# Two latents and two quarters of the tokens turned in 32x32 blocks by VectorE through DRAM instead of by TensorE

## The chip, the cores and the metric

One core of a Trainium2 chip runs the whole layer. The time is the device time in microseconds (us) of one execution, and a version's time is the median over its runs. In the text "the matrix engine" is TensorE (PE in the profile), VectorE is DVE, ScalarE is ACT, GpSimd is POOL and SyncE is SP.

## The reference, cut to what matters

One layer over 256 tokens (SEQ) of width 2048 in float32: a projection, two mixers side by side, a projection back, and a SwiGLU block.

```python
h    = rms_norm(x, attn_norm_w)
proj = h @ w_in                              # hq, hf, hi, hg (4 x 1024), c_q (512), c_kv (512), k_r (64)
o_a  = hgrn2_mixer(hq, hf, hi, hg, ...)      # gated linear recurrence, 8 heads of 128
q    = rms_norm(c_q, q_norm_w) @ w_uq        # the first latent, 256 x 512
kv   = rms_norm(c_kv, kv_norm_w) @ w_ukv     # the second latent, 256 x 512
o_b  = attention(q, kv, k_r)                 # 8 heads, rotary part from the positions
x    = x + concat([o_a, o_b]) @ w_out
h    = rms_norm(x, ffn_norm_w)
gate, up = split(h @ w_gate_up)              # 2 x 5632 columns
x    = x + (silu(gate) * up) @ w_down
```

## The kernel before

Tokens lie on the 128 partitions in two tiles (NT = 2, P = 128). A matrix product needs its token operand the other way round, features on partitions, so every activation that is multiplied has to be turned. The operands are split in two float32r parts, hi and lo, and a product is hi x hi + lo x hi + hi x lo: three matmuls per tile.

The weights come in **granules**: 256 weight rows by up to 512 columns, through a ring of four slots (`raw`). SP loads a granule, ACT makes `w_hi` (`convert`, L805), DVE makes `w_lo` (L1132), PE multiplies (L1751, L1754). 137 granules of the mixer and of `w_out` come first (G0 = 137), then the FFN, whose first block (16 granules, positions 137 to 152) still goes by the same loop; from the second block on it is a loop of another form.

The order of all work beside the granules is a table, `schedule()`: pairs of a position and a step. Each engine runs the same loop over positions g. ACT and DVE first convert granule g + 3 and then do their part of the steps at g; PE does its part of the steps at g and then multiplies granule g. So each engine is a strict queue, and ACT's cast of granule n waits until PE has finished granule n - 4 (the slot of `w_hi`). Turned tokens go through `SPLITS`, in schedule order: ACT makes the hi part and counts `s_thi`, DVE makes the lo part and counts `s_tlo`, and PE waits for `s_tlo`.

The steps that matter here, with their places:

- blocks of the mixer, in granules: lat (0 to 24), hq0 (25 to 32), uq0 (33, 34), hf0 (35 to 42), ukv0 (43, 44). `uq` multiplies the first latent, `ukv` the second; `split_needed` says what each block waits for.
- `lat_a`, `lat_b` (i = 0, 1): ACT squares a latent (L827), DVE takes mean and root and multiplies the latent by the result (L1260). `lat_in` copies the latent out of PSUM on DVE (L1253).
- `lat_t` (i, j): PE turns two blocks of 128 features for both tiles, four transposes against the identity (`turn_x`, L1793) into a PSUM bank, ACT and DVE split them into `mT_hi` and `mT_lo` (L852, L1153). Two such steps per latent, at positions 26 and 30.
- `angles` (DVE, about 20 small operations from L1194 to L1218) and `sines` (ACT, L870, with a table load before and one after) make the rotary factors, at positions 29 and 30.
- `hq` (ACT, L941): the first block read out of PSUM at position 33, again between two table loads. hf0 multiplies into the same banks and waits for it.
- `kr_b`, `q_a`, `q_b`, `q_t`: rotary key, norm and rotation of the first query block on DVE at 34 to 36; PE turns its result at position 39 (L1815), waiting for `s_stage`.
- `out1`, `out2` (c = 0 to 3): DVE adds the two parts of the `w_out` product to X (L1480). `out2` of quarter c (512 features) has two granules, and its addition stands at position 131 + 2c.
- `sq2`: ACT squares the quarter. `x2` (c, j): PE turns two blocks of the quarter, four transposes; ACT and DVE split them into `hT_hi` and `hT_lo`. Two such steps per quarter, at 133, 135, 137 and 139. Before the transposes PE waits until DVE has read `out2` of that quarter.

`hidden`, the result of an FFN block, is already turned another way: DVE turns 32x32 blocks (`turn_hidden`, L1533), POOL writes them to DRAM (`move_out`, L761) and reads them back in four DMAs (`move_in`, L767), one per row of blocks, so that the blocks come to their places.

```python
for g, (b, k, n) in enumerate(GRANULES):        # PE
    for s in steps_at(g):
        step(s)
    ...
    pe.wait_ge(s_tlo, split_needed(g))
    ...
    multiply(g % RING, g, lhs_of(kind, ks), 0, len(rows) - 1, main[b % 2], cols, ks)
```

Of the kernel before, what the change touches and what calls it, by code (L numbers as in the profile page):

```python
# [31 lines left out]
P = 128  # L32
# [182 lines left out]

Q = 32
# [3 lines left out]
def schedule():  # L220
# [52 lines left out]
    for c in range(4):  # L273
        s += [(END[("out1", c)], ("out1", c)), (END[("out2", c)], ("out2", c)), (END[("out2", c)] + 1, ("sq2", c))]
# [22 lines left out]
def side_uses(step):  # L297

    kind = step[0]
    if kind in ("x2", "lat_t", "o_t"):  # L300
        return [(step, "dve")]
# [24 lines left out]
SPLITS = [step for _, step in SCHEDULE if step[0] in ("x", "x2", "lat_t", "o_t", "attend")]  # L326
# [16 lines left out]
def split_needed(g):  # L343
# [5 lines left out]
    if kind == "uq":  # L349
        return SPLIT[("lat_t", 0, 1)] + 1  # L350
    if kind == "ukv":
        return SPLIT[("lat_t", 1, 1)] + 1
# [7 lines left out]
def hybrid_layer(nc, x, columns, positions, w_in, hgrn_lb, w_uq, w_ukv, q_head_norm_w, k_head_norm_w, w_out, w_gate_up,  # L360
# [7 lines left out]
    with ExitStack() as ctx:  # L368
# [80 lines left out]
        latents = (lat, hv)  # L449
        qTn = X[:, 0, :].rearrange("p (h t) -> p h t", h=HEADS)  # L450
# [8 lines left out]
        hiddenT = sb("hiddenT", [P, P // Q, SEQ])  # L459
        squares = nc.dram_tensor("squares", (P // Q, Q, P // Q, SEQ), F32, kind="Internal").ap()  # L460
# [17 lines left out]
        def turned(t):  # L478
            return hiddenT[:, :, :].rearrange("p a (t k r) -> p t k a r", t=NT, r=Q)[:, t, :, :, :]
# [24 lines left out]
        s_lat = sem("s_lat")  # L504
        s_sq = sem("s_sq")
# [18 lines left out]

        s_turned = sem("s_turned")
# [93 lines left out]
        def _(sp):  # L619
# [22 lines left out]
            for j in range(GU):  # L642
                half, k = divmod(j, KT // 2)
                slot = (G0 + j) % RING
# [47 lines left out]
        def _(pool):  # L692
# [57 lines left out]

            pool.wait_ge(s_lbused, 1)
# [4 lines left out]
            pool.dma_start(X[:, :, :], x_v).then_inc(s_xagain, 16)  # L756

# [38 lines left out]
        def _(act):  # L796
# [58 lines left out]
            def step(s):  # L855
# [26 lines left out]
                elif kind == "lat_t":  # L882
                    i, j = a
                    ps, k, col = filled(s), 4 * i + 2 * j, (V_KVN if i else V_QN) + 2 * j
                    split_hi([(mT_hi[:, k + n, :], ps[:, n * SEQ:(n + 1) * SEQ], col + n) for n in range(2)])
# [46 lines left out]
                elif kind in ("hq", "hf_a", "hi", "hg"):  # L932
# [3 lines left out]
                    if kind == "hq" and not a[0]:  # L936
                        act.wait_ge(s_side, USE[("lat_t", 0, 1)] + 1)
# [61 lines left out]
                elif kind == "x2":  # L999
                    ps, k = filled(s), 4 * a[0] + 2 * a[1]  # L1000
                    split_hi([(hT_hi[:, k + n, :], ps[:, n * SEQ:(n + 1) * SEQ], V_FFN + k + n) for n in range(2)])
                elif kind == "r2b":
                    root(("r2a",), NT)
# [115 lines left out]
        def _(dve):  # L1119
# [100 lines left out]
            def step(s):  # L1220
# [40 lines left out]
                elif kind == "lat_t":  # L1261
                    i, j = a
                    ps, k, col = filled(s), 4 * i + 2 * j, (V_KVN if i else V_QN) + 2 * j
                    split_lo(s, [(mT_lo[:, k + n, :], ps[:, n * SEQ:(n + 1) * SEQ], mT_hi[:, k + n, :], col + n)
                                 for n in range(2)])
# [204 lines left out]
                elif kind in ("out1", "out2"):  # L1470
# [7 lines left out]
                    for t in range(NT):  # L1478
                        v = X[:, t, c * NB:(c + 1) * NB]
                        tt(v, v, ps[t][:, :], ALU.add).then_inc(read, 1)  # L1480
                elif kind == "x2":
# [75 lines left out]
            def sum_ff_tokens():  # L1557
# [7 lines left out]
                dve.wait_ge(s_tlo, SPLIT[("x2", 0, 1)] + 1)  # L1565
# [171 lines left out]
        def _(pe):  # L1737
# [58 lines left out]
            def step(s):  # L1796
# [6 lines left out]
                elif kind == "lat_t":  # L1803
                    i, j = a
                    pe.wait_ge(s_const, N_IDENT)
                    pe.wait_ge(s_lat, NT * (i + 1))
                    turn_x(s, 2 * j, latents[i])
# [114 lines left out]

            for g, (b, k, n) in enumerate(GRANULES):
# [12 lines left out]
            for j in range(GU):  # L1936
# [3 lines left out]
                pe.wait_ge(s_tlo, SPLIT[("x2",) + divmod(min(j, 7), 2)] + 1)  # L1940
# [158 lines left out]
```

## Time and profile before

| | |
|---|---|
| median of three runs | 1108.75 us (1108.43 to 1109.88) |
| the profiled execution | 1108.98 us, its span 1107.3 us, so 1.7 us lie around the span |
| busy in the span | PE 1098.5 us (99%), DVE 899.7 (81%), ACT 644.6 (58%), POOL 60.3 (5%) |
| granted clock of PE | 1.00 throughout |
| DMA | 232 MB, mean 210 GB/s |

The page gives the busy time of each engine, the span in 40 slices, and the chain that ended last. The timeline lists single instructions with the idle time of their engine before them and what ended it; a row that stands for several instructions gives their count and the time from the first start to the last end. A PE row overlaps its successor: a granule's length is read from start to start.

### The profile page before, as it was taken

To read this page: it belongs to the slowest core of one execution; us is meant where nothing else is said; L and a number is where in the kernel's file an instruction comes from. 1 tells how busy PE (TensorE), PEld (TensorE's weight loads), DVE (VectorE), ACT (ScalarE), POOL (GpSimd) and SP (SyncE) were. 2 spreads that over 40 slices of the span, in tenths; PEclk is the share of its full clock that TensorE was granted. 3 is DMA by queue.
4 is the path that set the end of the run, shared out by engine and by line. 5 is a ranking of instruction groups with operands and counts; after the bars stand their busy time and mean duration, and the time that the engine had idled before them with its cause. 6 is when DMAs were issued, how large, how long until landed. Compare 5 with 4: busy or idle time off the path is not lost.

```text
span 1107.3 us, 15268 instructions
## 1 busy us (share of the span) xinstructions
PE 1098.5 (99%) x5142; PEld 924.2 (83%) x5142; DVE 899.7 (81%) x1237; ACT 644.6 (58%) x907; POOL 60.3 (5%) x154
## 2 busy tenths in 40 slices
PE   8999999999999999999999999999999999999998
PEld 7988888888888888888888888888888888888887
DVE  6688787587876576688888888988988889999887
ACT  6676776668654465355455455554554555654553
POOL 1500000000000000101100000010010010000000
PEclk9999999999999999999999999999999999999999
DMA  9966455555655465767777777777777787766665
GB/s 308 288 182 207 127 169 169 147 160 157 228 172 185 158 180 165 237 216 213 242 234 225 237 235 212 237 236 225 229 235 231 236 251 231 229 214 207 196 203 171
DMA packets 107411, 232.11 MB, mean 210 GB/s; under 512 B 8288, under 2 KB 17248, under 8 KB 107104
## 3 DMA queue, kind: packets, MB, share of 16 engines
q1 hardware_dynamic: 101360, 211.34, 61.3%
q0 software_dynamic: 5856, 19.93, 6.0%
q8 instruction: 28, 0.46, 0.2%
q10 hardware_dynamic: 144, 0.20, 0.1%
q14 instruction: 23, 0.19, 0.1%
HBM read 220.94 MB, written 10.49 MB: 209 GB/s over the span
## 4 chain that ended last, share of the span: by engine, by line
PE 93%; DVE 3%; DMA 2%; issue 1%; ACT 1%; SPq 0%; DVEq 0%; ACTq 0%
PE side L1979 22%; PE main L1751 22%; PE side L1981 11%; PE main L1754 11%; PE side L1949 4%; PE side L1950 4%; PE side L1951 4%; PE main L1951 3%; PE main L1949 3%; PE main L1950 3%; DMA raw<-in_w_down 1%; PE main L1771 1%; DVE w_lo L1590 1%; PE side L1877 1%; PE side L1793 1%
## 5 line engine op out<-in xcount | busy, mean ns | idle before, releaser
L1021 ACT CAST w_hi<-raw 128x1024 fp32r<-128x1024 f32 x245 | 239.6, 984 | 160.3 <-PE side L1979 61.1
L1590 DVE TENSOR_TENSOR w_lo<-raw,w_hi 128x1024 fp32r<-128x1024 f32 x245 | 274.5, 1133 | 17.1 <-ACT w_hi L1021 17.1
L1132 DVE TENSOR_TENSOR w_lo<-raw,w_hi 128x1024 fp32r<-128x1024 f32 (+3 forms) x156 | 178.9, 1156 | 96.1 <-ACT w_hi L805 94.5
L805 ACT CAST w_hi<-raw 128x1024 fp32r<-128x1024 f32 (+3 forms) x155 | 153.2, 997 | 127.2 <-PE main L1751 117.7
L1751 PE MATMUL main<-w_hi,hT_hi 128*128 128x512 f32 (+2 forms) x416 | 161.1, 388 | 0.0
L1754 PE MATMUL main<-w_hi,hT_lo 128*128 128x512 f32 (+2 forms) x416 | 157.6, 380 | 0.0
L1979 PE MATMUL side<-w_hi,hT_hi 128*128 128x512 f32 x400 | 155.6, 389 | 0.0
L1981 PE MATMUL side<-w_hi,hT_lo 128*128 128x512 f32 x400 | 155.6, 389 | 0.0
L1751 PE MATMUL main<-w_lo,hT_hi 128*128 128x512 f32 (+2 forms) x416 | 107.2, 379 | 0.0
L1979 PE MATMUL side<-w_lo,hT_hi 128*128 128x512 f32 x400 | 106.9, 389 | 0.0
L1754 PEld LDWEIGHTS main<-w_hi,hT_lo 128*128 128x128 f32 x416 | 78.2, 188 | 12.9
L1751 PEld LDWEIGHTS main<-w_hi,hT_hi 128*128 128x128 f32 x416 | 78.2, 188 | 12.9
L1751 PEld LDWEIGHTS main<-w_lo,hT_hi 128*128 128x128 f32 x416 | 76.8, 188 | 14.1
L1979 PEld LDWEIGHTS side<-w_hi,hT_hi 128*128 128x128 f32 x400 | 75.1, 188 | 15.6
L1979 PEld LDWEIGHTS side<-w_lo,hT_hi 128*128 128x128 f32 x400 | 75.1, 188 | 15.6
L1981 PEld LDWEIGHTS side<-w_hi,hT_lo 128*128 128x128 f32 x400 | 75.1, 188 | 15.5
L1590 DVE TENSOR_TENSOR w_lo<-last_two,w_hi 128x1024 fp32r<-128x1024 f32 x39 | 47.8, 1225 | 40.6 <-ACT w_hi L1021 40.5
L1021 ACT CAST w_hi<-last_two 128x1024 fp32r<-128x1024 f32 x39 | 41.1, 1053 | 64.5 <-PE side L1979 64.5
L1021 ACT CAST w_hi<-first_two 128x1024 fp32r<-128x1024 f32 x39 | 41.2, 1056 | 59.2 <-PE side L1979 57.3
L1979 PE MATMUL side<-w_hi,aT_hi 128*128 128x512 f32 x184 | 71.6, 389 | 0.0
L1981 PE MATMUL side<-w_hi,aT_lo 128*128 128x512 f32 x184 | 71.6, 389 | 0.0
L1751 PE MATMUL main<-w_hi,mT_hi 128*128 128x512 f32 (+1 forms) x160 | 62.0, 387 | 0.0
(295 smaller groups left out, 1877.1 us busy)
## 6 DMA issues: line engine op xcount, KB each, us to landing
raw<-in_w_gate_up SPq DMA_DIRECT2D x176, 512.0 KB, 4.8
raw<-in_w_down SPq DMA_DIRECT2D x88, 512.0 KB, 4.6
raw<-in_w_in SPq DMA_DIRECT2D x64, 512.0 KB, 4.3
raw<-in_w_out SPq DMA_DIRECT2D x32, 512.0 KB, 3.7
raw<-in_w_in SPq DMA_DIRECT2D x15, 384.0 KB, 5.5
squares<-hiddenT POOLq DMA_DIRECT2D x11, 512.0 KB, 5.2
hiddenT<-squares POOLq DMA_DIRECT2D x44, 128.0 KB, 5.4
raw<-in_w_ukv SPq DMA_DIRECT2D x8, 512.0 KB, 4.3
```

Of the source, the lines that this page charges most:

```text
L805: copy(w_hi[:, slot, 0:n], raw[:, slot, 0:n]).then_inc(s_hi, 1)
L1021: copy(w_hi[:, n % RING, 0:cols], src).then_inc(s_hi, 1)
L1132: tt(w_lo[:, slot, 0:n], raw[:, slot, 0:n], w_hi[:, slot, 0:n].bitcast(F32), ALU.subtract)\
L1590: tt(w_lo[:, n % RING, 0:cols], src, w_hi[:, n % RING, 0:cols].bitcast(F32), ALU.subtract)\
L1751: m = matmul(banks[t][:, 0:cols], hi[:, at[n], tok], rhs, start=(part == "hi" and k == k_first), stop=(part == "lo" and k == last))
L1754: matmul(banks[t][:, 0:cols], lo[:, at[n], tok], rhs, start=False, stop=False)
L1771: m = matmul(banks[t][:, 0:cols], tokens[:, k, t * P:(t + 1) * P], w[:, slot, n * cols:(n + 1) * cols], start=(part == "hi" and k == 0), s ...
L1949: matmul(bank, hi, big, start=first, stop=False)
L1950: matmul(bank, lo, big, start=False, stop=False)
L1951: return matmul(bank, hi, small, start=False, stop=last)
L1979: m = matmul(bank, hi, rhs, start=False, stop=(part == "lo" and (t, half) in last))
L1981: matmul(bank, lo, rhs, start=False, stop=False)
```

## The change

Four of the eight groups of eight transposes leave PE: both latents, and quarters 0 and 1 of the FFN's tokens. DVE turns them in 32x32 blocks out of SBUF, POOL writes the blocks to DRAM and reads them back in four DMAs, and ACT and DVE make hi and lo from SBUF instead of PSUM. The FFN's first block takes its quarters in the order 2, 0, 1, 3.

```diff
+FF_ORDER = [(c, n) for c in (2, 0, 1, 3) for n in range(2)]
...
-        s += [(e + 1, ("lat_a", i)), (e + 2, ("lat_b", i))] + [(e + 5, ("lat_t", i, n)) for n in range(2)]
+        s += [(e + 1, ("lat_a", i)), (e + 2, ("lat_b", i)), (e + 2, ("lat_turn", i))]
+        s += [(30 + n if i == 0 else 34, ("lat_back", i, n)) for n in range(2)]
...
-    s += [(END[("out2", c)] + 2, ("x2", c, n)) for c in range(4) for n in range(2)]
+    s += [(END[("out2", c)], ("x_turn", c)) for c in range(2)]
+    s += [(e + 2 * c, ("x_back", c, n)) for c in range(2) for n in range(2)]
+    s += [(e - 1 if c == 2 else e + 2, ("x2", c, n)) for c in range(2, 4) for n in range(2)]
...
     if kind == "uq":
-        return SPLIT[("lat_t", 0, 1)] + 1
+        return SPLIT[("lat_back", 0, 1)] + 1
...
+            for i in range(2):                                              # POOL
+                pool.wait_ge(s_latturned, i + 1)
+                pool.dma_start(lat_scratch[i].rearrange("a c b x -> (a c) b x"), latents_in_blocks[i])\
+                    .then_inc(s_latout[i], 16)
+                pool.wait_ge(s_latout[i], 16)
+                for b in range(P // Q):
+                    pool.dma_start(latents_in_blocks[i][Q * b:Q * (b + 1), :, :],
+                                   lat_scratch[i][:, :, b, :].rearrange("a c x -> c a x")).then_inc(s_latback[i], 16)
...
+            for c in range(2):
+                pool.wait_ge(s_xturned, NT * (c + 1))
+                pool.dma_start(x_scratch[c].rearrange("a c b x -> (a c) b x"), in_blocks(c)).then_inc(s_xout[c], 16)
+            for c in range(2):
+                pool.wait_ge(s_xout[c], 16)
+                for b in range(P // Q):
+                    pool.dma_start(in_blocks(c)[Q * b:Q * (b + 1), :, :],
+                                   x_scratch[c][:, :, b, :].rearrange("a c x -> c a x")).then_inc(s_xback[c], 16)
...
+                elif kind == "lat_back":                                    # ACT
+                    i, j = a
+                    act.wait_ge(s_latback[i], MOVED)
+                    src = latents_in_blocks[i].rearrange("p a (t k r) -> p k t a r", t=NT, r=Q)
+                    split_hi([(mT_hi[:, 4 * i + k, :].rearrange("p (t a r) -> p t a r", t=NT, r=Q), src[:, k, :, :, :],
+                               (V_KVN if i else V_QN) + k) for k in (2 * j, 2 * j + 1)])
...
+                elif kind == "lat_turn":                                    # DVE
+                    i = a[0]
+                    dve.wait_ge(s_lat, NT * (i + 1))
+                    nc.vector.transpose(latents_in_blocks[i].rearrange("p b (n r) -> p n b r", r=Q),
+                                        latents[i][:, :, :].rearrange("p t (k b c) -> p (t k) b c", b=P // Q, c=Q))\
+                        .then_inc(s_latturned, 1)
...
+                elif kind == "x_turn":                                      # DVE
+                    ...
+                    for t in range(NT):
+                        nc.vector.transpose(in_blocks(c).rearrange("p b (t k r) -> p t k b r", t=NT, r=Q)[:, t, :, :, :],
+                                            X[:, t, c * NB:(c + 1) * NB].rearrange("p (k b c) -> p k b c", b=P // Q, c=Q))\
+                            .then_inc(s_xturned, 1)
```

`x_back` is to a quarter what `lat_back` is to a latent. DVE's part of both makes four operations of 128x128 per step where `lat_t` and `x2` made two of 128x256. The blocks of the latents lie in `hkT` and `hgate`, those of the quarters in `hiddenT` and `hidden`. The wait of PE for the identity moves to the start of its loop.

**Where the instructions stand.** DVE around the first latent, positions 23 to 26 (`lat` is the first latent, `hv` the place of the second), before:

```order
L1260 TENSOR_SCALAR lat<-lat,opening 128x512 x2
L1132 TENSOR_TENSOR w_lo<-raw,w_hi 128x1024 x2
L1253 COPY hv<-main 128x256
L1251 TENSOR_SCALAR krw<-main,opening 128x64
L1253 COPY hv<-main 128x256
L1251 TENSOR_SCALAR krw<-main,opening 128x64
L1132 TENSOR_TENSOR w_lo<-raw,w_hi 128x1024
L1153 SCALAR_TENSOR_TENSOR mT_lo<-side,opening,mT_hi 128x256 x4
```

and with the change:

```order
L1305 TENSOR_SCALAR lat<-lat,opening 128x512 x2
L1309 STREAM_TRANSPOSE hkT<-lat 128x8x4x32
L1177 TENSOR_TENSOR w_lo<-raw,w_hi 128x1024 x2
L1298 COPY hv<-main 128x256
L1296 TENSOR_SCALAR krw<-main,opening 128x64
L1298 COPY hv<-main 128x256
L1296 TENSOR_SCALAR krw<-main,opening 128x64
L1177 TENSOR_TENSOR w_lo<-raw,w_hi 128x1024
```

The turning stands ahead of two weight granules and of the copies of the second latent; the lo part of the first latent is gone from here. The same turning of the second latent comes after its own multiplication.

ACT around the sines, positions 30 and 31 (the first two `mT_hi` rows of the change are `lat_back` of the first latent, halves 0 and 1), before:

```order
L805 CAST w_hi<-raw 128x768
L852 ACTIVATE mT_hi<-side,opening 128x256 x4
L870 ACT_TABLE_LOAD
L870 ACTIVATE sincos<-sincos 128x128
L844 ACT_TABLE_LOAD
L805 CAST w_hi<-raw 128x768
L805 CAST w_hi<-raw 128x1024 x2
```

and with the change:

```order
L842 CAST w_hi<-raw 128x768
L889 ACTIVATE mT_hi<-hkT,opening 128x256 x2
L907 ACT_TABLE_LOAD
L907 ACTIVATE sincos<-sincos 128x128
L881 ACT_TABLE_LOAD
L842 CAST w_hi<-raw 128x768
L889 ACTIVATE mT_hi<-hkT,opening 128x256 x2
L842 CAST w_hi<-raw 128x1024 x2
```

Before, these four made the second latent, needed at granule 43, and the first had been done at position 26; now they make the first latent, needed at granule 33, and its second half stands behind the sines and a cast. The second latent follows after `hq0`.

DVE at the end of `w_out`, positions 131 to 137, with the change (X additions are `out2` of quarters 0 to 3):

```order
L1539 TENSOR_TENSOR X<-X,main 128x512 x2
L1545 STREAM_TRANSPOSE hiddenT<-X 128x4x4x32 x2
L1177 TENSOR_TENSOR w_lo<-raw,w_hi 128x1024 x2
L1539 TENSOR_TENSOR X<-X,main 128x512 x2
L1545 STREAM_TRANSPOSE hidden<-X 128x4x4x32 x2
L1177 TENSOR_TENSOR w_lo<-raw,w_hi 128x1024 x2
L1539 TENSOR_TENSOR X<-X,main 128x512 x2
L1177 TENSOR_TENSOR w_lo<-raw,w_hi 128x1024
L1198 SCALAR_TENSOR_TENSOR hT_lo<-side,opening,hT_hi 128x256 x4
L1177 TENSOR_TENSOR w_lo<-raw,w_hi 128x1024
L1539 TENSOR_TENSOR X<-X,main 128x512 x2
L1557 SCALAR_TENSOR_TENSOR hT_lo<-hiddenT,opening,hT_hi 128x128 x8
```

The lo part of quarter 2 (`hT_lo<-side`) now comes one granule after the addition of that quarter, where before two `w_lo` and the addition of quarter 3 stood between.

## Rows read from the trace of the kernel before

**Rows 1.** The page, busy time of each engine, its share and instructions.
```profile
PE 1098.5 (99%) x5142; PEld 924.2 (83%) x5142; DVE 899.7 (81%) x1237; ACT 644.6 (58%) x907; POOL 60.3 (5%) x154
```
**Rows 2.** The waits of PE: line, for what; us in total, times, longest.
```profile
PE main L1771 <- ACTq L1058: 4.5, 1, 4.5
```
**Rows 3.** Timeline of PE: start us, us, line, instruction, tiles, count.
```profile
57.35 1.04 PE L1793 MATMUL side<-ident,lat 128*128 128x128 f32 x8
...
60.99 0.39 PE L1751 MATMUL main<-w_hi,hT_hi 128*128 128x512 f32 x1
...
78.21 0.33 PE L1751 MATMUL main<-w_hi,mT_hi 128*128 128x384 f32 x1
...
93.32 0.60 PE L1815 MATMUL side<-ident,stage 128*128 128x128 f32 x4
...
400.30 0.39 PE L1751 MATMUL main<-w_hi,hT_hi 128*128 128x512 f32 x1
...
403.02 1.03 PE L1793 MATMUL side<-ident,X 128*128 128x128 f32 x8
```
**Rows 4.** Instructions of L1533: duration ns min/median/max, first and last start.
```profile
L1533 DVE STREAM_TRANSPOSE hiddenT<-hidden x11: 1236/1239/1241, 457.3 to 881.2; 128x1024 f32<-128x1024 f32 x11
```
**Rows 5.** Timeline of DVE from the first latent to the sines.
```profile
55.07 0.88 DVE L1260 TENSOR_SCALAR lat<-lat,opening 128x512 f32<-128x512 f32 x2
...
58.14 0.42 DVE L1253 COPY hv<-main 128x256 f32<-128x256 f32 x1
...
60.32 0.88 DVE L1153 SCALAR_TENSOR_TENSOR mT_lo<-side,opening,mT_hi 128x256 fp32r<-128x256 f32 x2
...
65.32 0.88 DVE L1260 TENSOR_SCALAR hv<-hv,opening 128x512 f32<-128x512 f32 x2
...
67.77 1.22 DVE L1132 TENSOR_TENSOR w_lo<-raw,w_hi 128x1024 fp32r<-128x1024 f32 x1 [0.43 <-ACT w_hi L805]
68.91 0.16 DVE L1194 CAST pos_f<-pos_i 128x2 f32<-128x2 int32 x1
...
73.46 0.23 DVE L1218 TENSOR_SCALAR sincos<-sincos 128x128 f32<-128x128 f32 x1
73.60 0.95 DVE L1132 TENSOR_TENSOR w_lo<-raw,w_hi 128x768 fp32r<-128x768 f32 x1
```
**Rows 6.** Timeline of ACT from the second latent's squares to after `hq0`.
```profile
59.99 0.74 ACT L827 ACTIVATE hlf<-hv,opening 128x512 f32<-128x512 f32 x1
...
62.34 1.04 ACT L805 CAST w_hi<-raw 128x1024 fp32r<-128x1024 f32 x1
...
70.15 1.56 ACT L852 ACTIVATE mT_hi<-side,opening 128x256 fp32r<-128x256 f32 x4
...
74.04 1.28 ACT L844 ACT_TABLE_LOAD   x1
75.34 1.79 ACT L805 CAST w_hi<-raw 128x768 fp32r<-128x768 f32 x2
78.46 1.05 ACT L805 CAST w_hi<-raw 128x1024 fp32r<-128x1024 f32 x1 [1.34 <-PE main L1751]
...
83.41 2.00 ACT L805 CAST w_hi<-raw 128x1024 fp32r<-128x1024 f32 x2
```
**Rows 7.** Timeline of DVE from the granule after `uq0` to the first queries.
```profile
84.48 1.23 DVE L1132 TENSOR_TENSOR w_lo<-raw,w_hi 128x1024 fp32r<-128x1024 f32 x1 [2.75 <-ACT w_hi L805]
...
92.52 0.28 DVE L1188 TENSOR_TENSOR stage_r<-rot 128x128 f32<-128x128 f32 x1
```
**Rows 8.** Timeline of POOL at one turning of `hidden`, and landing times of these DMAs.
```profile
458.89 0.57 POOL L761 DMA_DIRECT2D squares<-hiddenT  x1 [169.34 <-DVE hiddenT L1533]
464.16 2.21 POOL L767 DMA_DIRECT2D hiddenT<-squares  x4 [4.70 <-DMA squares<-hiddenT]
...
DMA to landing us min/median/max: 3.6/5.3/7.8
```
**Rows 9.** Timeline of DVE, the addition of quarter 2.
```profile
405.50 1.28 DVE L1480 TENSOR_TENSOR X<-X,main 128x512 f32<-128x512 f32 x2
```

More of the change, by code:

```diff
@@ L299, in side_uses @@
     kind = step[0]
-    if kind in ("x2", "lat_t", "o_t"):
+    if kind in ("x2", "o_t"):
         return [(step, "dve")]
@@ L324 @@
             GIVEN[USE[_key]] = _given[_engine]
-SPLITS = [step for _, step in SCHEDULE if step[0] in ("x", "x2", "lat_t", "o_t", "attend")]
+SPLITS = [step for _, step in SCHEDULE if step[0] in ("x", "x2", "x_back", "lat_back", "o_t", "attend")]
 SPLIT = {step: n for n, step in enumerate(SPLITS)}
@@ L449, in hybrid_layer @@
         latents = (lat, hv)
+        latents_in_blocks = [v[:, :, :].rearrange("p t c -> p (t c)").rearrange("p (a x) -> p a x", a=P // Q)
+                             for v in (hkT, hgate)]
         qTn = X[:, 0, :].rearrange("p (h t) -> p h t", h=HEADS)
@@ L504, in hybrid_layer @@
         s_lat = sem("s_lat")
+        s_latturned = sem("s_latturned")
+        s_latout = [sem(f"s_latout{i}") for i in range(2)]
+        s_latback = [sem(f"s_latback{i}") for i in range(2)]
         s_sq = sem("s_sq")
@@ L523, in hybrid_layer @@
         s_join = sem("s_join")
+        s_xturned = sem("s_xturned")
+        s_xout = [sem(f"s_xout{c}") for c in range(2)]
+        s_xback = [sem(f"s_xback{c}") for c in range(2)]
         s_turned = sem("s_turned")
@@ L643, in _ @@
                 half, k = divmod(j, KT // 2)
+                k = 2 * FF_ORDER[k][0] + FF_ORDER[k][1]
                 slot = (G0 + j) % RING
@@ L1260, in step @@
                         ts(v, v, inv[:, t:t + 1], None, ALU.mult).then_inc(s_lat, 1)
-                elif kind == "lat_t":
-                    i, j = a
-                    ps, k, col = filled(s), 4 * i + 2 * j, (V_KVN if i else V_QN) + 2 * j
-                    split_lo(s, [(mT_lo[:, k + n, :], ps[:, n * SEQ:(n + 1) * SEQ], mT_hi[:, k + n, :], col + n)
-                                 for n in range(2)])
+                elif kind == "lat_turn":
[4 more added lines that the diff above has]
+                        .then_inc(s_latturned, 1)
+                elif kind == "lat_back":
+                    i, j = a
+                    dve.wait_ge(s_latback[i], MOVED)
+                    dve.wait_ge(s_thi, SPLIT[s] + 1)
+                    src = latents_in_blocks[i].rearrange("p a (t k r) -> p k t a r", t=NT, r=Q)
+                    for k in (2 * j, 2 * j + 1):
+                        col = (V_KVN if i else V_QN) + k
+                        for t in range(NT):
+                            hi, lo = [v[:, 4 * i + k, t * P:(t + 1) * P].rearrange("p (a r) -> p a r", r=Q)
+                                      for v in (mT_hi, mT_lo)]
+                            ins = stt(out=lo, in0=src[:, k, t, :, :], scalar=vec_cols[:, col:col + 1],
+                                      in1=hi.bitcast(F32), op0=ALU.mult, op1=ALU.subtract)
+                    ins.then_inc(s_tlo, 1)
                 elif kind == "kr_b":
```

60 lines of the change are left out of this document (41 added, 19 removed).

## The prediction

> **What bounds the kernel now.** I read the page first: PE is busy 1098.5 of 1107.3 us [rows 1], and of the 8.8 us that are left, 4.5 are its one real wait, for the first operands [rows 2]. So PE is the bound from end to end: what leaves its queue shortens the kernel by its own length, unless PE then arrives at something that isn't ready. The second reading is therefore not "who is busy" but "how much earlier than PE is each result there", and that takes the timelines of PE, DVE, ACT and POOL at the two places of the change [rows 3 to 9].
>
> **What is removed.** A granule that follows eight transposes starts 3.64 us after they start (57.35 to 60.99), one without them is 2.72 us long (400.30 to 403.02) [rows 3]. A group of eight costs 0.92 us. Four groups go: 2 x 0.92 = 1.84 us in the mixer, 1.84 us before the FFN, 3.7 us in all. That is the whole gain: 0.33% of the time.
>
> The Trainium skill ("VectorE: DVE Perf Modes", "The three transpose paths" and "Rules for kernel authors") speaks against the change: VectorE turns 32x32 blocks only, and a full 128x128 transpose belongs on TensorE where PSUM can take it. The rows agree on the durations: eight blocks take 1.24 us on DVE [rows 4] and 0.92 on PE. By the rule alone the sum would be four times 0.32, 1.3 us slower; by the rows what counts is whose queue is the bound, and where the new results are waited for.
>
> **The mixer, step by step.** I carry the times of the trace forward; up to 55.95, the end of the first latent's multiplication [rows 5], nothing differs.
> 1. DVE turns the first latent, same shape as the `hidden` block: 1.24 us [rows 4], to 57.2. Behind it stand two w_lo of 1.14 each (67.77 to 68.91) and the copies of the second latent (58.14 to 60.32 less one w_lo, 1.05) [rows 5]: copies done at 60.6, 1.3 us later than before.
> 2. ACT's squares of the second latent need these copies. They started at 59.99, held back until then by the hi part of the first latent that now is gone; now they start at 60.6, and the cast behind them at 62.95 instead of 62.34 [rows 6]. DVE waits for that cast, so the second latent's multiplication ends at 66.8 instead of 66.2 [rows 5].
> 3. DVE turns the second latent, 1.24 us, to 68.1; two w_lo to 70.3. The angles started at 68.91 and ran to 73.69 (73.46 + 0.23), 4.78 us [rows 5]. Now: 70.3 to 75.1, 1.4 us late. The lo part that left this stretch (twice 0.88 [rows 5]) had mostly stood in time in which DVE waits for casts anyway.
> 4. ACT's sine waits for the angles; from their end to the next cast passed 1.65 us (73.69 to 75.34: sine and a table load [rows 5, 6]). So that cast starts at 76.7. It is the cast of `uq0`'s second granule, and the second half of the first latent stands behind it on both engines. Its hi part follows 0.75 us behind that narrow cast and costs half of the four of the second latent, 0.86 us [rows 6]: 78.35. On DVE w_lo of 768 columns (0.95 [rows 5]) comes first, from 77.5 to 78.4, then the lo part, for which I take the 0.88 of the pair it replaces [rows 5]: 79.35.
> 5. PE reached `uq0` at 78.21 [rows 3], and would now at 76.37. It waits for the lo part until 79.35: **3.0 us of stall**, more than both groups of transposes gave.
> 6. Then the second latent, now behind `hq0`. ACT: hi to 78.3, one cast (0.95) to 79.25, then the 4.95 us from cast to cast across `hq0` (78.46 to 83.41 [rows 6]), so the cast of granule 37 starts at 84.2 and ends at 85.25. From this granule's w_lo to the first query block DVE ran without a pause, 84.48 to 92.80 [rows 7], 8.32 us; now the lo parts of the second latent are in it, 2 x 0.88. The block is there at 95.3. PE's transposes of it came 15.1 us after `uq0` (78.21 to 93.32 [rows 3]): 94.45. **Another 0.9 us.**
>
> Mixer: -1.84 + 3.0 + 0.9 = +2.1 us.
>
> The way through DRAM isn't on this path. `hidden` was turned at 458.54 (457.3 [rows 4] + 1.24); the write was issued at 458.89, the reads from 464.16 to 466.37, the last of them some 0.55 before that end [rows 8]. With the median of 5.3 us for its landing a latent is back 12.6 us after its turning: the first at 69.8, the second at 80.7. ACT needs the first by 72.9 (0.9 of hi and 1.3 of table load before the sine at 75.1), the second by 85. In POOL's queue they stand right after the masks of the opening, and nothing else waits behind them before the recurrence. SP's queue is untouched, and the added traffic, 0.5 MB out and 0.5 MB back per latent, meets loads that land well ahead of their casts: ACT waits for PE there, not for DMA [rows 6].
>
> What the operations from SBUF cost isn't in the trace. From below I set half of the replaced pair, from above the double: a stall of 2.1 to 4.7 us at `uq0`. I take the replaced rows, equal in elements.
>
> **Before the FFN.** DVE's additions of a quarter end 3.76 us after PE has started the granule behind the quarter: 405.50 + 1.28 = 406.78 against 403.02 [rows 3, 9]. ACT's cast (it waits for PE's slot), w_lo and the two additions make that up, and the change leaves them as they are; the turnings of quarters 0 and 1 come one position earlier, in time where DVE waited. But quarter 2's transposes now stand one granule after the quarter, 2.72 us, not two. PE waits until the additions are done: **1.05 us of stall**. With it, quarter 2 is split in time: PE needs it 3.6 us after the transposes start, and four transposes (0.5), hi (0.86), lo (0.88) and the steps between the engines take some 2.6.
>
> Quarter 0, counted from the start of granule 133: turned (1.25 us after its addition) at -0.4, written by 5.2; POOL first sends quarter 1 (turned at 5.0), then issues the reads from 5.9 to 8.1, landed by 12.9. PE starts granule 137 at 12.85 (four granules, the stall, one group of transposes), and ACT has a cast and two squares before it: about 15.7. Quarter 1 is written by 10.7, back at 17.6, and ACT comes to it near 21. Both hidden, with 2.8 us of room. PE's sum tiles use quarter 0 alone, much later.
>
> Before the FFN: -1.84 + 1.05 = -0.8 us. The reordered quarters load the same bytes, and the identity is made long before PE's first matmul: both nothing.
>
> **Sum.** +2.1 - 0.8 = +1.3 us on the profiled execution's 1108.98, so 1110.3; that execution lies 0.2 above the median of its runs, so 1110.0 for a median. Its own range, from the bounds above: with the cheap SBUF operations 1108.2 (both stalls of the mixer shrink, the second to nothing), with the dear ones 1111.8. A measurement of this kernel can tell about 0.2%, 2.2 us, from no change: 1106.5 to 1111.0 is "the same".
>
> **Rivals.**
> - *All of it comes through*: 1108.75 - 3.7 = 1105.1. For it: PE has no wait anywhere now, DVE still waits 0.43 us for a cast in this very stretch [rows 5] and is only 81% busy. Against it: PE arrives 1.84 us earlier at everything, while sine and angles are later by 1.4. And even with the latents for nothing, the mixer can't give it: from the cast at 76.7 ACT has two casts and, from the second on, 3.65 us to the end of the `hq0` read (78.46 to 83.41 less a table load of 1.30 [rows 6]), done 82.05, and hf0 (82.44 before, 93.32 less four granules) can't start sooner, 80.6 being PE's time. That would be 1107.5. 0.12 for a gain of over 2.2.
> - *The latent comes back late.* Such DMAs land in 3.6 to 7.8 us [rows 8]. If write and last read both take 7.8, the first latent is back at 74.8 instead of 69.8. ACT, which stands at it with sine, table load and cast queued behind, then gets to the sine at 77.0 instead of 75.1, and `uq0` waits 1.9 us more: 1111.9, slower. It decides from 72.9 on, and costs its own lateness from there; 73.9 makes it measurable. For it: two DMAs one after the other, beside the weights' queue. Against: the median gives 3 us of room. 0.12.
> - *The forecast*: 0.76, of which 0.08 lie above 1111.0 (the dear SBUF operations).
>
> So faster 0.12, same 0.68, slower 0.20. The range of 8 in 10 reaches from 1107.0, below which only the first rival lies, to 1112.2, which holds the second.
>
> **What would show it.** In the profile of the changed kernel, PE has three new waits where it had none: about 3 us at the first matmul on `mT_hi` (`uq0`, near 76.4) for DVE's `mT_lo`, about 0.9 at the query transposes for `stage_r`, about 1 before the transposes of X for DVE's addition. The angles end near 75.1, ACT's `mT_hi` rows from `hkT` take 0.4 to 0.5 us each, and the first of them doesn't wait for a DMA. Transposes drop from 8 groups of x8 on L1793's successor to 4 (the two of the recurrence's output stay beside the two quarters). I am wrong if PE runs into `uq0` without a wait, or if ACT waits for `hkT`'s DMA past 73, or if a stall turns up where I have none, at hf0 or at the FFN's third granule.

## The result, and the profile after

| | before | after |
|---|---|---|
| median of the timed runs | 1108.97 us (8 runs, 1108.43 to 1109.88) | 1113.03 us (8 runs, 1110.98 to 1115.08) |
| profiled execution, its span | 1108.98, 1107.3 us | 1113.29, 1111.5 us |

The ratio is 1.0033, with a 95% interval of 1.0024 to 1.0042. The changed kernel is slower by 0.33%, or 3.7 us (4.1 between the medians), where the forecast had 1.3, and the median lies 0.8 us above the upper end of the range.

The first look is at the busy times on the page; they answer to [rows 1]. PE's 32 transposes are gone, and it is busy for as long as before, in a longer span:

```profile
PE 1098.4 (99%) x5110; PEld 924.5 (83%) x5110; DVE 906.6 (82%) x1259; ACT 646.0 (58%) x907; POOL 71.2 (6%) x174
```

So what left PE's queue came back as slower matmuls. The second look is at PE's waits (line, for what; us in total, times, longest), against [rows 2]:

```profile
PE main L1850 <- ACTq L1103: 4.4, 1, 4.4
PE main L1830 <- DVE mT_lo L1322: 3.1, 1, 3.1
PE side L1872 <- DVE X L1539: 0.9, 1, 0.9
PE main L1850 <- ACT hT_hi L889: 0.7, 1, 0.7
```

The second row is the forecast's wait at `uq0`, the third its wait ahead of quarter 2. The forecast's wait at the query transposes is not there. To see where the 4.2 us of span come from, I took the start of the same instruction in both traces at five points, and the end of both spans; the column "later by" is the difference.

| point | before | after | later by |
|---|---|---|---|
| first matmul after the opening (granule 9) | 23.88 | 26.00 | 2.12 |
| first matmul of `uq0` | 78.21 | 81.73 | 3.52 |
| first matmul of `hf0` | 82.39 | 87.60 | 5.21 |
| query transposes | 93.32 | 98.52 | 5.20 |
| table load of the FFN's first Silu | 434.25 | 438.78 | 4.53 |
| end of the span | 1107.3 | 1111.5 | 4.2 |

**Two things the forecast hadn't.** One lies ahead of everything the change touches. The timeline of PE in the opening of the changed kernel (start us, us, line, instruction, tiles, count):

```profile
7.76 0.84 PE L1850 MATMUL main<-w_lo,hT_hi 128*128 128x384 f32 x2
9.28 1.62 PE L1850 MATMUL main<-w_hi,hT_hi 128*128 128x384 f32 x4 [0.68 <-ACT hT_hi L889]
10.69 1.49 PE L1850 MATMUL main<-w_hi,hT_lo 128*128 128x384 f32 x4
11.97 1.49 PE L1850 MATMUL main<-w_lo,hT_hi 128*128 128x384 f32 x4
13.25 1.10 PE L1850 MATMUL main<-w_hi,hT_hi 128*128 128x384 f32 x4
14.19 0.88 PE L1850 MATMUL main<-w_hi,hT_lo 128*128 128x384 f32 x4
```

and the same stretch before:

```profile
7.94 0.82 PE L1771 MATMUL main<-w_lo,hT_hi 128*128 128x384 f32 x2
8.96 0.94 PE L1771 MATMUL main<-w_hi,hT_hi 128*128 128x384 f32 x4 [0.20 <-ACT hT_hi L852]
9.78 0.97 PE L1771 MATMUL main<-w_hi,hT_lo 128*128 128x384 f32 x4
10.59 0.85 PE L1771 MATMUL main<-w_lo,hT_hi 128*128 128x384 f32 x4
11.28 0.85 PE L1771 MATMUL main<-w_hi,hT_hi 128*128 128x384 f32 x4
```

Four matmuls take 1.28 us from start to start (10.69 to 11.97), and 0.69 before (10.59 to 11.28): 0.32 us for 384 columns against 0.173. These are the two levels of the clock, 1.2 and 2.4 GHz. Both kernels start at the lower one; after, PE stays on it some 4 us longer. The Trainium skill ("TensorE: Matmul & The Clock Gate", Part 1: The HAM clock gate) says that the length of the slow start differs from run to run of one kernel; whether that is so here is for the runs below to tell.

The other is behind the wait at `uq0`. PE's timeline there (the wait is in brackets):

```profile
81.73 0.45 PE L1830 MATMUL main<-w_hi,mT_hi 128*128 128x384 f32 x1 [3.06 <-DVE mT_lo L1322]
...
83.58 0.52 PE L1830 MATMUL main<-w_hi,mT_hi 128*128 128x384 f32 x1
83.90 0.52 PE L1833 MATMUL main<-w_hi,mT_lo 128*128 128x384 f32 x1
84.22 1.43 PE L1830 MATMUL main<-w_lo,mT_hi 128*128 128x384 f32 x4
85.48 0.34 PE L1830 MATMUL main<-w_hi,mT_hi 128*128 128x384 f32 x1
...
87.60 0.39 PE L1830 MATMUL main<-w_hi,hT_hi 128*128 128x512 f32 x1
```

The first granule of `uq0` takes 3.75 us (81.73 to 85.48), the second 2.12. Before, the two took 4.18 together (78.21 to 82.39); now 5.87. The granted clock says why; the windows of that stretch, whose columns are PE, weight loads, DVE, ACT and POOL busy, the clock, DMA share and GB/s:

```profile
76.00:78.60 2.60, 2.60 (x12) 1.88 (x10) 2.50 (x8) 1.42 (x2) 1.08 (x2) 1.00 0.96 264
78.60:81.70 3.10, 0.07 (x1) 0.00 (x0) 2.47 (x8) 3.09 (x6) 0.00 (x0) 1.00 0.65 190
81.70:85.40 3.70, 3.67 (x12) 3.67 (x13) 3.67 (x5) 3.65 (x5) 0.00 (x0) 0.54 0.84 238
85.40:88.00 2.60, 2.60 (x15) 2.56 (x15) 1.18 (x2) 2.59 (x5) 0.00 (x0) 0.99 0.50 143
```

0.54 behind the wait, 1.00 ahead of it. The wait costs its 3.06 us and then another 1.69 (5.87 less 4.18).

**The chain that makes the wait is the forecast's.** The timelines of DVE and ACT, to be held against [rows 5, 6]; 2.1 us of each start are the opening's:

```profile
72.33 0.16 DVE L1239 CAST pos_f<-pos_i 128x2 f32<-128x2 int32 x1
...
76.88 0.26 DVE L1263 TENSOR_SCALAR sincos<-sincos 128x128 f32<-128x128 f32 x1
...
79.65 0.96 DVE L1177 TENSOR_TENSOR w_lo<-raw,w_hi 128x768 fp32r<-128x768 f32 x1 [0.63 <-ACT w_hi L842]
80.53 1.14 DVE L1322 SCALAR_TENSOR_TENSOR mT_lo<-hkT,opening,mT_hi 128x128 fp32r<-128x128 f32 x4
```

```profile
72.21 0.84 ACT L842 CAST w_hi<-raw 128x768 fp32r<-128x768 f32 x1 [3.27 <-DMA raw<-in_w_uq]
...
77.17 0.31 ACT L907 ACTIVATE sincos<-sincos 128x128 f32<-128x128 f32 x1 [2.01 <-DVE sincos L1263]
77.50 1.28 ACT L881 ACT_TABLE_LOAD   x1
78.79 0.83 ACT L842 CAST w_hi<-raw 128x768 fp32r<-128x768 f32 x1
79.53 0.91 ACT L889 ACTIVATE mT_hi<-hkT,opening 128x256 fp32r<-128x256 f32 x2
```

The angles start at 70.2 when the 2.12 of the opening are taken off (forecast 70.3), end at 75.0 (75.1), the cast starts at 76.7 (76.7) and the lo part ends at 79.5 (79.35). The way through DRAM is hidden: no row of PE, ACT or DVE in the mixer waits for `hkT` or `hgate` from DRAM (in a second profile of this kernel ACT waits 0.22 us for `hkT`, ahead of 2.79 us for the angles). But a cast waits 3.27 us for its load, where ACT in the trace of before waited for PE; it costs nothing, since ACT waits another 2.01 for the angles behind it.

### The profile page after: what moved, and what is told of

Same layout as the page of the kernel before. It is cut to its first block, busy times and chain, and to the rows that moved or that the text cites. A ratio compares the mean times of both kernels' runs of the same rounds, so it can differ in the third digit from the quotient of the medians.

```text
span 1111.5 us, 15220 instructions
## 1 busy us (share of the span) xinstructions
PE 1098.4 (99%) x5110; PEld 924.5 (83%) x5110; DVE 906.6 (82%) x1259; ACT 646.0 (58%) x907; POOL 71.2 (6%) x174
## 4 chain that ended last, share of the span: by engine, by line
PE 91%; DVE 4%; ACT 2%; issue 1%; DMA 0%; SPq 0%; DVEq 0%; ACTq 0%
PE side L2057 24%; PE main L1830 19%; PE side L2059 12%; PE main L1833 9%; PE side L2027 4%; PE side L2028 4%; PE side L2029 4%; PE main L2029 3%; PE main L2027 3%; PE main L2028 3%; PE main L1850 2%; DVE w_lo L1177 1%; PE side L1951 1%; ACT w_hi L842 1%; DMA x_columns<-in_columns 0%
## 5 line engine op out<-in xcount | busy, mean ns | idle before, releaser
L1177 DVE TENSOR_TENSOR w_lo<-raw,w_hi 128x1024 fp32r<-128x1024 f32 (+3 forms) x156 | 178.5, 1154 | 95.3 <-ACT w_hi L842 94.2
L2057 PEld LDWEIGHTS side<-w_hi,hT_hi 128*128 128x128 f32 x400 | 75.1, 188 | 15.6
L2057 PEld LDWEIGHTS side<-w_lo,hT_hi 128*128 128x128 f32 x400 | 75.1, 188 | 15.6
L2059 PEld LDWEIGHTS side<-w_hi,hT_lo 128*128 128x128 f32 x400 | 75.1, 188 | 15.6
```

The source lines that it names most:

```text
L1177: tt(w_lo[:, slot, 0:n], raw[:, slot, 0:n], w_hi[:, slot, 0:n].bitcast(F32), ALU.subtract)\
L2057: m = matmul(bank, hi, rhs, start=False, stop=(part == "lo" and (t, half) in last))
L2059: matmul(bank, lo, rhs, start=False, stop=False)
```

## The experiments

Every time is compared with runs of the kernel before on the same chip. "later by" is as above, the start of an instruction less that in the profile of before.

**The two parts apart, and the wait that moved.** Four kernels: the latents alone (`x2` and the FFN's order as before), the quarters alone (`lat_t` as before), and PE's wait for the identity, which the change puts at the start of PE's loop, elsewhere:

```diff
-            pe.wait_ge(s_const, N_IDENT)
             for g, (b, k, n) in enumerate(GRANULES):
...
                 elif kind in ("q_t", "k_t"):
                     j, b = a[0], int(kind == "k_t")
+                    pe.wait_ge(s_const, N_IDENT)
```

and in the fourth the kernel before with that wait moved to the start of the loop. Latents alone:

> Only the two latents are turned by VectorE; X, the FFN's order and the position of quarter 2 are as before. Theory: the mixer alone loses 3.1 us (1.84 us of transposes gone, 3.2 of wait at uq0, 1.7 because TensorE works at the lower clock level behind that wait), so 3.1 us above the kernel before where PE's ninth granule starts as early as there (23.9 us), and 2.1 more in runs where the opening is late (26.0). Rival, the forecast's own step: 3.0 at uq0 and 0.9 at the query transposes, 2.1 us above. Rival on the opening: it comes from the change (identity wait, new DRAM tensors), so it is late here too in most runs.

Quarters alone:

> Only quarters 0 and 1 of X are turned by VectorE, with the FFN's first block in the order 2, 0, 1, 3; the latents are transposed by TensorE as before. Theory: the FFN part gains 0.7 us (1.84 less a wait of 0.9 and 0.2 of seams), so 0.7 us below the kernel before if the opening is early. Rival on the opening: if the new identity wait or a new DRAM tensor makes it late, 1.4 us above, with PE's ninth granule at 26.0.

Wait late:

> The whole change, but PE's wait for the identity stands ahead of the query transposes instead of at the start of its loop. Theory (opening is a matter of when the first loads land): same as the changed kernel, 1111 to 1113, in both kinds of opening. Rival (that wait delays the opening): ninth granule at 23.9 in every run and 1111.0, 2 us below the changed kernel.

Before, with the wait early:

> The kernel before with nothing changed but the place of PE's wait for the identity, now at the start of its loop. Theory: no difference from the kernel before, 1109. Rival (that wait delays the opening): ninth granule at 26.0 and 2.1 us above, 1111.1.

The changed kernel itself was run once more:

> The changed kernel once more, to see its opening. Theory (the late opening of the first profile was the order in which the first loads landed): ninth granule near 23.9 us in this profile, wait at uq0 3.0, median 1111.5 to 1112.5, 2.4 us above the kernel before plus what late openings add. Rival (the opening belongs to the change): ninth granule at 26.0 again and 4 us above.

| kernel | median, us | ratio to before (95%) | granule 9 starts | later by at `uq0` | `hf0` | queries | Silu |
|---|---|---|---|---|---|---|---|
| latents alone | 1112.04 | 1.0022 (1.0010 to 1.0033) | 24.00 | 1.48 | 3.13 | 3.12 | 3.11 |
| quarters alone | 1108.57 | 0.9993 (0.9983 to 1.0002) | 24.21 | 0.31 | 0.32 | 0.32 | -0.38 |
| wait late | 1112.18 | 1.0023 (1.0013 to 1.0033) | 24.02 | 1.50 | 3.17 | 3.18 | 2.42 |
| before, wait early | 1108.81 | 0.9994 (0.9984 to 1.0004) | 23.74 | -0.14 | -0.13 | -0.13 | -0.18 |
| changed kernel again | 1112.89 | 1.0029 (1.0017 to 1.0040) | 23.96 | 1.44 | 2.99 | 2.99 | 2.25 |

The late opening isn't in the changed kernel's second profile (23.96), nor in any other of this study: it stood in one of the fifteen profiles, before and after among them, and neither the latents, nor the quarters, nor the wait for the identity brought it in the one profile that each of these kernels has. The same kernel shows 26.00 and 23.96: the length of the slow start does differ from run to run of one kernel here. The rest repeats: the latents cost 3.0 to 3.2 us by the query transposes, the quarters gain 0.7 from there to the Silu. These two make 2.3 to 2.4 us, and the kernel with the wait late measured 0.23%, 2.6 us (its interval: 1.4 to 3.7). The times alone tell less than the profiles: the latents' 0.22% (1.1 to 3.7 us) holds the 3.1 us of the theory and the 2.1 of its rival, and the quarters' 0.07% isn't clear of no change. The changed kernel's own medians lie 3.8 to 4.1 us above the kernel before, its ratios 3.2 (1.9 to 4.4) and 3.7 (2.7 to 4.7). In its second profile the surplus over 2.4 is late, from 2.25 us at the Silu to 3.8 at the end, with two waits of the later block for 1.1 of it:

```profile
PE side L2027 <- DVE w_lo L1669: 0.7, 1, 0.7
PE side L2027 <- DVE gate L1607: 0.4, 1, 0.4
```

Such a wait stands in other profiles too (0.7 in the kernel before with the wait early, 0.5 in the quarters alone), so it doesn't belong to the change. Whether the changed kernel has late openings or late waits more often than the others stays open: a timed run leaves no profile.

**Is it the clock?** PE is kept at work through most of the wait with transposes of the identity, into the bank that `uq0` overwrites; their results are used nowhere:

```diff
-                pe.wait_ge(s_tlo, split_needed(g))
                 if k == 0 and b >= 2:
                     pe.wait_ge(s_taken[b % 2], taken(b - 2))
+                if (kind, i, k) == ("uq", 0, 0):
+                    for _ in range(24):
+                        transpose(main[b % 2][0][:, 0:P], ident[:, :], ident[:, :])
+                pe.wait_ge(s_tlo, split_needed(g))
```

> The changed kernel with 24 transposes of the identity, 0.11 us each, in TensorE's queue ahead of its wait at uq0, into the bank that uq0 is about to overwrite; they compute nothing that is used. They fill 2.6 of the 3.0 us of wait. Theory (TensorE's clock falls because of the wait, and that costs 1.7 us behind it): uq0's two granules take 4.2 us instead of 5.85; the query transposes then wait for VectorE, 0.9 us, as the forecast had it; 0.8 us below the changed kernel. Rival (uq0 is slow for another reason, its operands or the DMA traffic): 5.85 us again, and no change of the time.

PE's timeline of that kernel:

```profile
76.39 2.78 PE L2010 MATMUL main<-ident 128*128 128x128 f32 x24
79.68 0.45 PE L1830 MATMUL main<-w_hi,mT_hi 128*128 128x384 f32 x1 [0.51 <-DVE mT_lo L1322]
...
81.89 0.33 PE L1830 MATMUL main<-w_hi,mT_hi 128*128 128x384 f32 x1
...
83.97 0.39 PE L1830 MATMUL main<-w_hi,hT_hi 128*128 128x512 f32 x1
...
95.72 0.66 PE L1889 MATMUL side<-ident,stage 128*128 128x128 f32 x4 [0.67 <-DVE stage_r L1233]
```

`uq0` takes 4.29 us at a granted clock of 1.00, with the same operands ready at the same time; in the five profiles that have the whole wait it takes 5.73 to 5.87, and 4.18 before. So the clock cost 1.6 to 1.7 us. And the wait at the query transposes, which the forecast had and the changed kernel had not, is there: 0.67, so that much of the clock's cost only took the place of a wait that would have come anyway. PE comes to the query transposes 0.59 us earlier than in the changed kernel's second profile (95.72 against 96.31). The kernel measured 1111.01 (ratio 1.0016, 1.0006 to 1.0026) against 1112.89, which is more than the profile shows and more than the expected 0.8.

The timed runs bear the clock out, for each left its span and its mean granted clock. The fall of the first profile, 0.54 for 3.7 us, makes a mean of 0.998. Five kernels or series have the whole wait: the changed kernel twice, the latents alone, the wait late, and the early quarter 2 of below. Of their 42 runs 35 read 0.996 to 0.998, while all 90 runs of the other nine kernels here and 100 runs of the kernel before read 0.999 or 1.000. The seven that read 1.000 have spans 0.6 to 2.7 us below the median of their kernel's other runs. In the first series of the changed kernel five of eight runs read 0.996 or 0.997, against three of 34 in the other four. An estimate from these means (at most 0.9975, over a span of 1111 us): such a run lost at least 2.8 us to the clock, 1.1 more than the 1.7 of the profile's one fall. Where it lost them isn't recorded.

**What is late next?** One word lets each granule of `uq0` wait for its own half of the latent:

```diff
     if kind == "uq":
-        return SPLIT[("lat_back", 0, 1)] + 1
+        return SPLIT[("lat_back", 0, k // 2)] + 1
```

> The changed kernel, but uq0's first granule waits only for the half of the first latent that it uses (both granules waited for both halves). Theory: two waits of some 0.5 us in place of one of 3.0, and no fall of the clock. What is late next holds TensorE: the read of hq0 on ACT (ends at 82.8 in the times of the trace of before) and the query block on VectorE (95.6). So waits of some 1 to 2 us at hf0 and at the query transposes, and no more than 0.9 us below the changed kernel. Rival (the wait at uq0 is the whole loss): 3.6 to 4.3 us below the changed kernel, 1 to 2 below the kernel before.

PE's timeline, the rows with a wait:

```profile
76.85 0.44 PE L1830 MATMUL main<-w_hi,mT_hi 128*128 128x384 f32 x1 [0.40 <-DVE mT_lo L1322]
...
79.47 0.45 PE L1830 MATMUL main<-w_hi,mT_hi 128*128 128x384 f32 x1 [0.25 <-DVE mT_lo L1322]
...
82.74 0.47 PE L1830 MATMUL main<-w_hi,hT_hi 128*128 128x512 f32 x1 [0.91 <-issue]
...
95.51 0.66 PE L1889 MATMUL side<-ident,stage 128*128 128x128 f32 x4 [1.47 <-DVE stage_r L1233]
```

A wait of 3.0 us and the clock's 1.7 go from `uq0`, and PE comes to the query transposes 0.80 us earlier than in the changed kernel (95.51 against 96.31 in its second profile), within the expected 0.9; the medians differ by 1.4. Two results that were late all along hold it: `hq0`'s read on ACT (0.91; it ends at 82.64 in this profile) and the query block on DVE (1.47). The kernel measured 1111.51 (ratio 1.0021). The whole stretch is late, not one operand.

**The wait ahead of quarter 2.**

```diff
-(END[("out2", c)], ("out2", c))
+(END[("out2", c)] - (c == 2), ("out2", c))
```

> The changed kernel, but VectorE adds quarter 2 to X before the low part of the weights of granule 138 instead of after it. Theory: the additions end 1.2 us earlier, the wait of 0.9 us ahead of quarter 2's transposes goes, 0.9 us below the changed kernel. Rival (the wait moves to the next operand, the low part of quarter 2 or of granule 138's weights): a new wait of up to 0.9 us at the FFN's first granules, and no change.

PE's timeline: the transposes of quarter 2 in the changed kernel's first profile,

```profile
411.10 1.09 PE L1872 MATMUL side<-ident,X 128*128 128x128 f32 x8 [0.94 <-DVE X L1539]
```

and with the early addition:

```profile
407.57 1.04 PE L1872 MATMUL side<-ident,X 128*128 128x128 f32 x8
```

The wait is gone and no other takes its place. From the query transposes to the Silu pass 339.06 us, against 340.19 in the changed kernel's second profile and 340.93 before. Median 1110.36 (ratio 1.0012), 2.5 below the changed kernel, where 0.9 was expected; the profile's FFN part accounts for 1.1 of them.

**Taking the chain away.** Next the work that made the latent late leaves the stretch. The angles are cut in four pieces and made earlier, the sine stands where ACT waits for a DMA, the second latent's parts come behind the query block:

```diff
-("angles",)), (e + 5, ("sines",)), (e + 9, ("kr_b",))]
+(29, ("sines",)), (e + 9, ("kr_b",))]
+    s += [(at, ("angles", n)) for n, at in enumerate((18, 19, 20, 21))]
...
-(30 + n if i == 0 else 34, ("lat_back", i, n))
+(30 + n if i == 0 else 37, ("lat_back", i, n))
```

The small loads that the angles need go out two granules earlier (`SMALL_AFTER` 18), and their wait for POOL's constants covers only the frequencies.

> The changed kernel, but the angles (4.8 us of VectorE) are made in four pieces behind positions 18 to 21, where VectorE waits for casts, the sine with its two table loads stands at position 29, where ACT waits for a DMA, and the second latent's parts are made at position 37, behind the query block. Theory (the chain turnings, angles, sine, table, cast is what makes the second half of the first latent late): no wait at uq0, none at the query transposes, no fall of the clock; the mixer gains its 1.84 us, with the FFN's 0.7 that makes 2.5 below the kernel before, 1106.5. Rival (the way through DRAM or ACT's slots bound the latent): a wait of 1 us or more at uq0 for DVE's mT_lo stays, or a new one at hf0, and the time isn't below the kernel before.

Together with the two edits above:

> As the run with the early angles, with quarter 2 added to X early and with each granule of uq0 waiting for its own half. Theory: all four groups of transposes come through, 3.7 us below the kernel before, 1105.3. Rival: a wait of 0.5 us or more remains somewhere in the mixer and it is less than 2 us below.

And the quarters alone, with the early addition:

> The latents by TensorE as before; quarters 0 and 1 turned by VectorE, and quarter 2 added to X early. Theory: the two groups of the FFN come through, 1.84 us below the kernel before less 0.2 of seams, 1107.3. Rival (a new wait at the FFN's first granules takes the place): 0.7 below or less.

| kernel | median, us | ratio to before (95%) | granule 9 starts | later by at `uq0` | `hf0` | queries | Silu |
|---|---|---|---|---|---|---|---|
| early angles | 1107.81 | 0.9985 (0.9976 to 0.9994) | 23.77 | -1.93 | -1.53 | -1.47 | -2.17 |
| and own halves, early quarter 2 | 1107.26 | 0.9982 (0.9973 to 0.9991) | 24.34 | -1.31 | -0.23 | -0.18 | -2.02 |
| quarters alone, early quarter 2 | 1107.12 | 0.9984 (0.9975 to 0.9993) | 23.94 | 0.06 | 0.06 | 0.06 | -1.66 |

With the chain gone, PE enters `uq0` 1.93 us earlier and without a wait: the 1.84 of two groups of transposes and 0.11 of the opening. (Angles, sine and the second latent's parts moved together; which of them it took wasn't tried.) All three are faster than before. The first was expected at 2.5 below: its span is 2.5 us shorter, but its median only 1.3 lower (1.7 by the ratio). In its profile 2.7 us lie around the span instead of 1.7. That figure is 2.4 to 3.0 in 20 of the 94 runs of kernels with both parts, and at most 1.8 in all runs of the kernel before and of the kernels with one part; its cause is open.

The third came out as expected (1107.3). The second misses its 3.7 and goes as its rival had it, 1.8 below by the medians: a wait remains at `hf0`, 0.91 us, again for `hq0`'s read. ACT's timeline shows what stands ahead of that read:

```profile
76.58 1.05 ACT L843 CAST w_hi<-raw 128x1024 fp32r<-128x1024 f32 x1 [1.41 <-DMA raw<-in_w_in]
78.42 1.05 ACT L843 CAST w_hi<-raw 128x1024 fp32r<-128x1024 f32 x1 [0.79 <-DMA raw<-in_w_in]
79.50 1.28 ACT L981 ACT_TABLE_LOAD   x1
80.79 1.27 ACT L981 ACTIVATE lat<-main,opening 128x512 f32<-128x512 f32 x2
```

Two casts wait for their loads, in the time in which the second latent goes out and back (issued at 70.0, read from 74.1 on). ACT also came to them late: a cast ahead of the sine had already waited 1.07 us for its load. That gives two more kernels: `hq0`'s read one position earlier, ahead of the second of these casts, with the table load behind it; and the second latent held back until that cast is done (and its parts at position 40):

```diff
                 pool.wait_ge(s_latturned, i + 1)
+                if i:
+                    pool.wait_ge(s_hi, 37)
```

> The version with early angles, own halves and early quarter 2, but ACT reads hq0 one position earlier, ahead of the cast of granule 36, and loads the table back behind that cast. Theory (hf0 waits for this read, which stands behind a cast that waits for its DMA): the wait of 0.2 to 0.9 us at hf0 goes, and the time falls by as much, to 3 us or more below the kernel before. Rival (granule 36's cast is now late instead): a wait of 0.5 us at hf0's second granule, no change.

> The version with early angles, own halves and early quarter 2, but the second latent is sent to DRAM only when granule 36 is cast, and its parts are made at position 40. Theory (its megabyte delays the loads of w_in that ACT waits for): ACT's waits for these loads ahead of the casts of granules 35 and 36 (2.2 to 2.7 us together with the megabyte) fall under 0.5, and the wait at hf0 goes. Rival (these loads are late because their slots come free late): the waits stay as they are.

| kernel | median, us | ratio to before (95%) | granule 9 starts | later by at `uq0` | `hf0` | queries | Silu |
|---|---|---|---|---|---|---|---|
| early read of `hq0` | 1106.42 | 0.9971 (0.9959 to 0.9982) | 24.15 | -1.56 | -1.55 | -1.56 | -3.33 |
| second latent held back | 1106.66 | 0.9980 (0.9970 to 0.9990) | 23.81 | -1.82 | -1.82 | -1.82 | -3.21 |

Both remove the wait at `hf0`. With the second latent held back, ACT's two casts read

```profile
74.84 1.05 ACT L845 CAST w_hi<-raw 128x1024 fp32r<-128x1024 f32 x1 [1.40 <-DMA raw<-in_w_in]
76.64 1.06 ACT L845 CAST w_hi<-raw 128x1024 fp32r<-128x1024 f32 x1 [0.75 <-PE main L1843]
```

These waits are as long as in the kernel without the hold (1.41 and 0.79). They end 1.7 us earlier, but ACT also comes to them 1.7 us earlier, so this pair doesn't show what the traffic did. The kernel with the early angles alone is the fairer measure, for there ACT comes to the first cast at the same time within 0.1 us:

```profile
75.77 1.05 ACT L843 CAST w_hi<-raw 128x1024 fp32r<-128x1024 f32 x1 [2.40 <-DMA raw<-in_w_in]
```

With the latent held back that cast waits 1.40 instead of 2.40, and the second one waits for its slot and no longer for its load. So part of the lateness may be the latent's traffic, on one profile of each; the expectation of under 0.5 for both fell. The early read of `hq0` has the lowest median of the study, 0.29% below before: 3.33 us ahead at the Silu, of the four groups' 3.7, with an opening that was 0.27 later. The intervals of the two overlap, so which of them is faster isn't shown.

## Why the prediction was wrong

- *What is removed* (four groups of 0.92 us) was right: `uq0` comes 1.75 to 1.83 us early where nothing else is late, once the opening's difference is taken off, and the FFN's part gains 1.4 to 1.9 (340.93 before, 339.06 to 339.54 in the kernels with the early addition).
- *Mixer, steps 1 to 5* were right: angles, sine, cast and a wait of 3.0 us at `uq0` (3.06 and 3.02). The hi part of two took 0.91 (0.86 taken). The lo part took 1.14, not 0.88: four operations on 128x128 from SBUF cost more than two on 128x256 from PSUM with equal elements. The part ended 0.2 us later than forecast.
- *Mixer, step 6 and the sum, "-1.84 + 3.0 + 0.9 = +2.1"*, failed in one term: "PE's transposes of it came 15.1 us after `uq0`". PE was taken to go on behind the wait at the pace it had before it. It went on at the lower clock level, and the transposes came 16.7 to 16.8 us after `uq0` in the five profiles with the wait: 1.6 to 1.7 us more, behind which the wait of 0.9 at the queries vanished. The query block itself was there at 95.6, forecast 95.3. Filling the wait brought the pace back and the other wait with it. Instead of 2.1, the mixer lost 3.0 to 3.2. The Trainium skill's page "TensorE: Matmul & The Clock Gate" (Part 1) says that the clock follows how busy TensorE has lately been; the trace agrees (0.54 behind the wait, 1.00 with the wait filled). A term for the slower matmuls was missing from the sum.
- *Before the FFN*: 0.94 of wait for 1.05, and a gain of 0.7 for 0.8. Right.
- *The way through DRAM is not on the path*: right for the changed kernel. "Meets loads that land well ahead of their casts" was wrong: one cast waited 3.27 us for its load, at no cost as long as the angles were later still; in the kernels with the early angles such waits reached PE at `hf0`.
- *"Up to 55.95 nothing differs"* failed in the profiled execution: its opening was 2.1 us longer. No part of the change does that in the other profiles, so it isn't shown to be a term of the sum, but it is a spread that the range left out, as it left out waits of 0.4 to 0.7 us in the later block, 1.1 together in one profile.

The mechanisms make 2.3 to 2.4 us, about 1111.3, inside the range. So the failed term alone would not have carried the time out of the range. Between 1111.3 and the median of 1113.0 lie 1.7 us. The profiles show two sources of that size, the opening and the late waits, in one profile each; the timed runs show a third, at least 1.1 us more at the lower clock in five of the eight. Which of them made the median stays open.

## What to carry to other kernels

Where TensorE is the bound, a wait of some microseconds can cost more than its length, here 3.0 us and then 1.6 to 1.7: read the granted clock and the pace of the matmuls behind it, and give the slow matmuls a term of their own. And before work goes from TensorE to an engine that has idle time, look at what stands behind the new instructions in that engine's order; here it was 4.8 us of angles that could as well be made 20 us earlier (they end at 53.1 with the early angles, at 73.7 before), and only with these out of the way did moving the latents pay: 1.5 to 1.8 us at the query transposes, in the profiles of the three kernels whose wait at `hf0` is 0.23 us or none. The times are less sure of the latents' share, for the intervals of the quarters alone with the early quarter 2 (0.9975 to 0.9993) and of the best kernel with both (0.9959 to 0.9982) overlap. Removing the named wait alone is worth little while the results next in line are as late: lengthen the view to the next two or three.

## What the hardware showed that I had not expected

- The granted clock reads 1.00 in the opening, in both kernels, where 384 columns take 0.32 us instead of 0.173: there the level shows only in the starts of the matmuls, and a reading of 1.00 doesn't stand for the full pace. Behind the wait at `uq0` column and pace agree.
- Waits of 0.40, 0.25, 0.91 and 1.47 us, with work between them, left the clock at 1.00. The one of 3.0 to 3.1 didn't in any of its five profiles, though 7 of 42 timed runs with it read 1.000. Nor does the fall come at a fixed place: with the wait late, PE went on at 79.71 and read 1.00 from 80 to 81 us, then 0.54 from 81 to 82.
- 24 transposes that compute nothing made the kernel faster than it was without them (1111.01 against 1112.89; the profiles show 0.59 us of that at the query transposes).
